# Scores of a head pair issued together in two row halves, with four bias strips, in a four-layer transformer kernel

## The reference, cut to what matters

```python
# the same pattern in moba, diff, dil (causal) and na (all 512 keys), per head h
s = einsum('bhqd,bhkd->bhqk', q, k) * 64 ** -0.5 + bias      # 64-wide contraction
s = where(mask, s, NEG)
p = softmax(s, axis=-1)
o = einsum('bhqk,bhkd->bhqd', p, v)
```

## Time and profile before

| | us |
|---|---|
| median of 3 runs | 3389.32 (3382.71 to 3393.28) |
| the profiled execution | 3389.83 |
| its span, first to last instruction | 3388.0 |
| PE busy | 3214.5 (95%) |
| POOL, DVE, ACT busy | 1659.5, 1544.9, 781.1 |

### The profile page before, as it was taken

How to read it: one execution, slowest core, us unless ns; L and a number is a source line. 1 busy time by engine, 2 the same in 40 slices (tenths; PEclk the granted TensorE clock), 3 DMA queues, 4 the chain that set the end, 5 groups by cost and what they waited for, 6 DMA issues and landing times.

```text
span 3388.0 us, 44988 instructions
## 1 busy us (share of the span) xinstructions
PE 3214.5 (95%) x14378; PEld 2530.7 (75%) x14378; DVE 1544.9 (46%) x2780; ACT 781.1 (23%) x1419; POOL 1659.5 (49%) x1254
## 2 busy tenths in 40 slices
PE   7998999999899998899999979998899999989996
PEld 5776888877688887667778858887667778868885
DVE  3335444333454434533334476633633334476634
ACT  2323221013322212142321122201142311122201
POOL 4233666662166665313246646674313256636673
PEclk9999999999999998789999989998789999979998
DMA  5225233321023232112222212232102213212232
GB/s 131 72 72 151 93 99 102 108 88 56 26 87 99 93 112 87 38 31 54 78 66 93 90 56 99 93 114 72 38 31 54 78 66 102 87 56 96 96 109 71
DMA packets 99596, 274.78 MB, mean 81 GB/s; under 512 B 38126, under 2 KB 38894, under 8 KB 99490
## 3 DMA queue, kind: packets, MB, share of 16 engines
q1 hardware_dynamic: 96176, 268.41, 24.8%
q10 hardware_dynamic: 3314, 5.02, 0.7%
HBM read 269.66 MB, written 11.54 MB: 83 GB/s over the span
## 4 chain that ended last, share of the span: by engine, by line
PE 70%; DVE 4%; ACT 1%; issue 1%; DVEq 0%; ACTq 0%
PE PA L453 10%; PE PA L455 10%; PE PA L454 10%; PE PB L453 8%; PE PB L455 8%; PE PB L454 8%; PE O L576 4%; PE S L632 3%; PE T L570 2%; PE S L539 2%; DVE acc L1194 1%; PE O L491 1%; DVE strip L1566 0%; DVE tmp L1223 0%; PE O L483 0%
## 5 line engine op out<-in xcount | busy, mean ns | idle before, releaser
L435 POOL TENSOR_TENSOR wl<-raw,wh 128x1024 fp32r<-128x1024 f32 (+2 forms) x416 | 1125.1, 2705 | 33.4
L432 POOL TENSOR_TENSOR zero<-zero 128x1 f32<-128x1 f32 x416 | 82.3, 198 | 1653.6 <-PE PA L455 799.4
L453 PE MATMUL PA<-hh,wh 128*128 128x512 f32 x1392 | 568.8, 409 | 33.9 <-DVE hl L1188 16.8
L455 PE MATMUL PA<-hh,wl 128*128 128x512 f32 x1392 | 552.6, 397 | 0.0
L454 PE MATMUL PA<-hl,wh 128*128 128x512 f32 x1392 | 552.5, 397 | 0.0
L433 POOL CAST wh<-raw 128x1024 fp32r<-128x1024 f32 (+2 forms) x416 | 478.3, 1150 | 0.0
L453 PEld LDWEIGHTS PA<-hh,wh 128*128 128x128 f32 x1392 | 266.9, 192 | 158.0 <-issue 79.0
L453 PE MATMUL PB<-hh,wh 128*128 128x512 f32 x896 | 365.0, 407 | 0.0
L454 PE MATMUL PB<-hl,wh 128*128 128x512 f32 x896 | 354.8, 396 | 0.0
L455 PE MATMUL PB<-hh,wl 128*128 128x512 f32 x896 | 354.6, 396 | 0.0
L455 PEld LDWEIGHTS PA<-hh,wl 128*128 128x128 f32 x1392 | 267.6, 192 | 58.1
(11 more groups left out here) (262 smaller groups left out, 5135.6 us busy)
## 6 DMA issues: line engine op xcount, KB each, us to landing
raw<-in_w_up SPq DMA_DIRECT2D x176, 512.0 KB, 3.4
raw<-in_w_down SPq DMA_DIRECT2D x64, 768.0 KB, 4.2
raw<-in_w_merge SPq DMA_DIRECT2D x48, 768.0 KB, 4.2
raw<-in_w_out SPq DMA_DIRECT2D x32, 512.0 KB, 3.5
strips_na<-in_rpb SPq DMA_DIRECT2D x1, 7620.0 KB, 32.0
strip<-strips_na SPq DMA_DIRECT2D x32, 224.0 KB, 4.0
strip<-strips_rel SPq DMA_DIRECT2D x96, 64.0 KB, 1.9
raw<-in_w_pool SPq DMA_DIRECT2D x12, 512.0 KB, 3.4
```

What stands on the lines that cost most here:

```text
L435: nc.gpsimd.tensor_tensor(wl[s][:, 0:width], raw[s][:, 0:width], wh[s][:, 0:width].bitcast(F), ALU.subtract).then_inc(w_split, 1)
L453: mm(dst, h_, rh, start=first, stop=False)
L455: return mm(dst, l_, rh, start=False, stop=last)
```

## The change

Within a group, unit `t` is now head `t % 2`, query tile `t // 2 % 4`. PE issues the scores of units `t` and `t+1` together at even `t`, for the same query tile of both heads, head 0 always into S0 and head 1 always into S1. The order of transposes, fill and products is otherwise that of before, by unit number. In a causal stage the units of a group now have 1, 1, 2, 2, 3, 3, 4, 4 blocks of keys.

Both strips of a group are needed from its first unit on, so a second pair of strips is made of `tmp[0]` to `tmp[3]`: even groups use `strip`, odd ones the new pair, each with its own semaphore. Their loads wait for 0, 1, 8 and 16 units taken. In `na` DVE masks the strips of the next group at `t % 8 == 4` and 5, and two of them ahead of the loop. `y_squares` writes `tmp[1]` in place of `tmp[0]`.

```diff
-        tmp = [sb(f"tmp{i}", [P, S]) for i in range(5)]
+        tmps = sb("tmps", [P, 5, S])
+        tmp = [tmps[:, i, :] for i in range(5)]
...
+        strips_at = strip, [tmps[:, 2 * i:2 * i + 2, :].rearrange("p a n -> p (a n)") for i in range(2)]
...
-                sp.wait_ge(s_taken, b["u"] + 2 if i == 0 else b["u"] + 8 * i + 4 * s - 2)
+                sp.wait_ge(s_taken, b["u"] + 2 + (0, 1, 8, 16)[i])
+                at = strips_at[i % 2][s]
...
                 def span(t):
-                    return S if full else (t % 4 + 1) * P
+                    return S if full else (t // 2 % 4 + 1) * P
+
+                def score(t):
+                    g, head, qt = t // 8, t % 2, t // 2 % 4
...
+                    if t < 2:
+                        pe.wait_ge(v_copied, 4 * b["v"] - 3 + t)
+                    pe.wait_ge(s_taken, u + t + 1)
+                    r = slice(64 * head, 64 * head + 64)
+                    mm(SB[head][:, 0:span(t)], queries[g % 2][r, qt * P:qt * P + P], keys[g % 2][r, 0:span(t)],
+                       start=True, stop=True).then_inc(s_ready, 1)
 
                 for t in range(end + 1):
-                    if t < 32:
...
-                        mm(SB[t % 2][:, 0:span(t)], queries[g % 2][r, qt * P:qt * P + P], keys[g % 2][r, 0:span(t)],
-                           start=True, stop=True).then_inc(s_ready, 1)
+                    if t < 32 and t % 2 == 0:
+                        score(t); score(t + 1)
                     if t in turns:
                         y_turn(b, turns.index(t), kind)
...
                 if full:
-                    mask_strip(0, arrived(0))
+                    mask_strip(0, 0, arrived(0)); mask_strip(0, 1, arrived(0))
                 for t in range(turns[3] + 3):
-                    g, head, qt = t // 8, t // 4 % 2, t % 4
-                    if full and t < 32 and t % 8 == 2:
-                        mask_strip(1, arrived(g))
-                    if full and t < 24 and t % 8 == 6:
-                        mask_strip(0, arrived(g + 1))
+                    g, head, qt = t // 8, t % 2, t // 2 % 4
+                    if full and t < 24 and t % 8 in (4, 5):
+                        mask_strip(g + 1, head, arrived(g + 1))
```

More of the change, by code:

```diff
@@ L70, in counts @@
     elif kind in ("causal", "na", "diff"):
-        c.update(a=3, b=3, u=32, g=4, st=4 * STRIP_PARTS[kind], d=4 * UNIT_LINKS[kind], df=4 if kind == "diff" else 0)
+        c.update(a=3, b=3, u=32, g=4, st=2 * STRIP_PARTS[kind], d=4 * UNIT_LINKS[kind], df=4 if kind == "diff" else 0)
     elif kind == "axial":
@@ L292, in build @@
         yt_ready, y_hi, y_split = sem("yt_ready"), sem("y_hi"), sem("y_split")
-        strip_in = [sem("strip_in0"), sem("strip_in1")]
+        strip_in = [[sem(f"strip_in{i}{s}") for s in range(2)] for i in range(2)]
         v_ready, v_copied = sem("v_ready"), sem("v_copied")
@@ L616, in span @@
                 def span(t):
-                    return S if full else (t % 4 + 1) * P
-                for t in range(end + 1):
-                    if t < 32:
-                        g, head, qt = t // 8, t // 4 % 2, t % 4
[L622 to L631, removed]
-                        mm(SB[t % 2][:, 0:span(t)], queries[g % 2][r, qt * P:qt * P + P], keys[g % 2][r, 0:span(t)],
-                           start=True, stop=True).then_inc(s_ready, 1)
+                    return S if full else (t // 2 % 4 + 1) * P
+                def score(t):
+                    g, head, qt = t // 8, t % 2, t // 2 % 4
+                    if t == 0:
+                        pe.wait_ge(pa_taken, b0["a"] + 2)
+                        pe.wait_ge(pb_taken, b0["b"] + 2)
+                    elif t % 8 == 0:
+                        pe.wait_ge(pa_taken, b["a"] + g + 1)
+                        pe.wait_ge(pb_taken, b["b"] + g + 1)
+                    if t < 2:
[4 more added lines that the diff above has]
+                       start=True, stop=True).then_inc(s_ready, 1)
+                for t in range(end + 1):
+                    if t < 32 and t % 2 == 0:
+                        score(t); score(t + 1)
                     if t in turns:
@@ L1303, in y_scale @@
             def y_scale(b, t, kind):
-                u, g, qt, c = b["u"], t // 8, t % 4, t % 8
-                if kind == "diff" and c >= 4:
+                u, g, qt, c, head = b["u"], t // 8, t // 2 % 4, t % 8, t % 2
+                if kind == "diff" and head:
                     link(TT(lrd[:, c:c + 1], rden[:, c:c + 1], neglam, ALU.mult))
@@ L1310, in y_scale @@
                 if kind != "diff":
-                    at = 64 * (c // 4)
+                    at = 64 * head
                     TS(y[:, at:at + 64], OB[t % 2][:, 0:64], rden[:, c:c + 1], None, ALU.mult).then_inc(o_taken, 1)
-                elif c < 4:
+                elif not head:
                     TS(y, OB[t % 2][:, 0:P], rden[:, c:c + 1], None, ALU.mult).then_inc(o_taken, 1)
@@ L1335, in y_norm, with mask_strip @@
                         ins.then_inc(y_normed, 1)
-            def mask_strip(head, at):
-                dve.wait_ge(strip_in[head], at)
-                st = strip[head][:, :].rearrange("p (j k) -> p j k", j=14)
+            def mask_strip(g, head, at):
+                dve.wait_ge(strip_in[g % 2][head], at)
+                st = strips_at[g % 2][head][:, 0:STRIP].rearrange("p (j k) -> p j k", j=14)
                 link(STT(out=st, in0=st, scalar=-1.0,
@@ L1363, in attention @@
                 if full:
[L1364 removed]
+                    mask_strip(0, 0, arrived(0)); mask_strip(0, 1, arrived(0))
                 for t in range(turns[3] + 3):
[L1366 to L1370 removed]
+                    g, head, qt = t // 8, t % 2, t // 2 % 4
+                    if full and t < 24 and t % 8 in (4, 5):
+                        mask_strip(g + 1, head, arrived(g + 1))
                     if t < 32:
                         if not full and qt == 0:
[L1373 removed]
+                            dve.wait_ge(strip_in[g % 2][head], arrived(g))
                         L = S if full else (qt + 1) * P
                         at = (6 - 2 * qt) * 64 if full else (3 - qt) * P
[L1376 removed]
+                        score(u, t, kind, L, strips_at[g % 2][head][:, at:at + L])
                     if 0 <= t - 2 < 32:
```

18 lines of the change are left out of this document (9 added, 9 removed).

## The result

| | before | after |
|---|---|---|
| median on the same chip | 3391.30 (4 runs, 3382.71 to 3393.53) | 3331.89 (4 runs, 3330.12 to 3332.65) |
| the profiled execution | 3389.83 | 3332.25 |
| its span | 3388.0 | 3330.4 |

The ratio is 0.9829, 95% interval 0.981 to 0.9847: faster by 59 us, 57.6 between the two profiled executions. The direction and two scores running at once were forecast; how much of them runs at once was not, and 3331.9 lies under the low end, 3337.

What follows compares the result with a forecast made beforehand. PE was taken to bound the kernel, busy 95% of the span. From 3389.83 us, 49.5 saved (22.9 visits, 26.6 overlap) and 7.6 of stalls added gave 3347.9, stated as 3348; range 3337 to 3379.

Steps and rivals of the forecast that it cites:

- The serial rival: Paired score passes on PE don't overlap, so the row halves do nothing: 3374.5 to 3382.5 us; chance 0.18.
- The clock's rival: Idle spells in odd steps without fill lower the granted clock, 34 us lost, 3416 with serial passes; chance 0.05.
- Part 1: In five attention stages 80 odd steps lose their separate score visit on PE: 22.9 us saved.
- behind: PE's extra time after a score, before fill matmuls run at their usual spacing: 0.11 us per visit.
- Part 2: Passes of a pair's two scores run at once in different row halves of PE: 26.6 us saved.
- A high, A low, B high, B low: PE's assumed pass order in a pair of two-pass scores A and B; only A low and B high overlap.
- from below: Bound on a pair's time on PE: one whole pass hidden per pair, no open load, 26.6 us together.
- keeps: Half of the 0.19 us inside a score, put on the second pass's weight load: 0.10 us not saved per visit.
- Part 3: New PE stalls in odd steps without fill, where a product waits for ACT's copy: 7.6 us lost.
- Steps 15 and 23: In causal stages `y_turn`'s four transposes fill 0.43 us, leaving a 0.29 us stall each; in `na` covered.
- The second mask of `na`: A 1.1 us mask on DVE before the first unit, hidden by six parts of fill (4.2 us): no cost.
- The ends of `moba`, `diff` and `dil`: Stalls in the last odd steps: `moba` 0.85, `diff` 0.15 and 0.72, `dil` 1.2 us.

Runs made afterwards that it cites:

- experiment 2: The kernel before, own unit order, with scores of units t and t+1 issued together at even t, both in the same 64 rows: 3372.78 us.
- experiment 1: The changed kernel (new numbering, strips and masks) with each score issued alone in its own step again: 3384.67 us.
- experiment 3: The changed kernel with the squares, root and norm of `diff` one step earlier: 3320.44 us.
- experiment 9: The changed kernel with both first masks of `na` ahead of the value copy on DVE: 3324.67 us.
- experiment 6: The changed kernel with the earlier norm in `diff`, ACT's copy ahead of its exponential in even steps, and `y_turn` last in its step: 3308.81 us.
- experiments 4: The changed kernel with ACT's copy of unit t-2 ahead of the exponential of unit t in even attention steps: 3332.01 us.
- 5: The changed kernel with `y_turn` last in its step, behind fill, transposes and product: 3332.12 us.
- 10: The changed kernel with the edits of experiment 6, scores paired in `axial` too, and the mask move of experiment 9: 3301.18 us.

## Where the prediction held, and why it was short by 16 us

**The mechanism held.** PE bounds the five stages, the row halves run side by side (experiment 2 against the change: 41 us), halving the visits helps on its own (16 us), and nothing else in the change matters (experiment 1). What failed is the size of the overlap and of what it gives back. The serial rival had 3374.5 to 3382.5; experiment 2 has that case, pairs whose passes don't overlap, and took 3372.8. The clock's rival had its mechanism in `diff` alone, two falls that cost about 1.4 us each where about ten were needed.

**Part 1** stands but for 4.7 of its 22.9 us. The way in and out of a pair are those of a single score, and experiment 2, net of its stalls, gained 16. But in an odd step with fill the first fill matmul now follows products instead of a score, and its neighbour starts 0.31 behind it instead of 0.23. Timeline of PE in `dil`:

```profile
797.97 1.00 PE L579 MATMUL O<-V,probsT 128*128 128x64 f32 x8
798.79 0.48 PE L456 MATMUL PB<-hh,wh 128*128 128x512 f32 x1
799.10 0.40 PE L457 MATMUL PB<-hl,wh 128*128 128x512 f32 x1
```

So of the 0.11 "behind" only 0.03 went: 59 x 0.08 = 4.7.

**Part 2 is the step that failed.** "In a pair the order is A high, A low, B high, B low", and so "one whole pass is hidden per pair". The order is not that: both heads start within 7 ns and both of B's passes are hidden, with both of its loads. A score is one matmul of the program; its two passes follow each other within its own row half and hold up nothing in the other. The bound "from below" was none: 26.6 was taken as the most that could be hidden. It is 26.6 twice, and the 0.10 that a visit "keeps" for its load was not kept for B, 80 x 0.10 = 8.0. With the 4.7 of Part 1 taken off, the gross gain worked out is 49.5 + 26.6 + 8.0 - 4.7 = 79.4.

The Trainium skill (TensorE: Matmul & The Clock Gate, The cost: per-tile semaphore tail) has increments serialize at about 26 ns each, which would have made it 2 us worse. The trace has such a tail, but PE doesn't pay it: the second increment of a pair comes 42 or 43 ns behind the first, where the passes end 7 ns apart, while a pair with two increments takes PE 1.06 and a score with one 1.05.

**Part 3 was three times too small**: 79.4 - 57.6 = 21.8 us given back, idle or at the lower clock, against 7.6. What the runs show of it:

- The wait for ACT's copy in step 7 was there: 0.8 in each causal stage (worked out: 0.72) and 0.2 in `na` (0.34), 2.8 in all.
- Steps 15 and 23 were priced at 0.29. They cost 1.0 in `moba`, `dil` and `diff`, 0.4 in `na`, because of K. This is the sentence "K is taken at DVE's step 6, and PE waits for it at step 8": step 8 was checked, but `y_turn`, which stands one step ahead of it and needs the same bank, was not. Together some 7.6 us where 1.7 was in the sum.
- In `diff` the same wait is 2.8 us, since `y_norm` on DVE, which no part of the forecast names, stands ahead of `take_k` and takes 3.8 us beside POOL's split instead of 1.3, and the clock falls behind it: 6.3 us more (experiment 3).
- The second mask of `na`, at nothing because "six parts of fill (4.2 us) lie between": two masks took 4.69 us instead of 2.2, since POOL's split runs beside them. 1.5 us in each `na`, 3.0 (experiment 9). The other masks (steps 4 and 5) collide in the same way and cost nothing, since DVE has time there.

That is 2.8 + 7.6 + 6.3 + 3.0 = 19.7 of the 21.8. The ends of `moba`, `diff` and `dil`, 2.9 in the forecast, are the rest: by PE's waits there before and after they cost 1.6, about nothing and 0.4.

A second balance agrees: 17.4 us more of idle time in the five stages, and an estimate of 4 us from the mean granted clock of the two profiled executions, 0.956 and 0.954 (0.046 of 3330.4 us less 0.044 of 3388.0). From 79.4 that leaves 58.0, against 57.6 measured.

Experiments 6 and 9 together took 19.3 + 3.0 us out of the stages by four small moves, so nearly all of it was a matter of order, not of work.

The two errors went in opposite directions: 34.6 - 4.7 = 29.9 too little gross, 14.2 too little given back. The rest, 15.7, is the miss between the sum (3347.9) and the profiled execution. That the number came so near is in part luck: each of the two errors alone would have put it 14 or 30 us off. The range's low end allowed for stalls of nothing and one hidden pass, and for no size of the gross gain above it.

## What to carry to other kernels

Fp32 matmuls that contract over 64 rows should be issued in twos, one for each half of the rows, where PE sets the pace: here the second cost nothing, passes and loads included. Where other engines are close behind, as in `axial`, less than half of PE's saving arrives (6.5 of 16.9 us). When a stage is shortened by some microseconds in steps that carry little else, follow each bank that PE writes back to the instruction that frees it, in every step, and look for what else stands ahead of that instruction, and at which of DVE's instructions will now run beside POOL's. And two mends that each show nothing in the time (experiments 4 and 5) may be worth over 10 us together, so they should be tried together before they are given up: experiment 6 less experiment 3 is 11.6 us in the medians and 13.9 in the stages, where the stages of 4 and 5 alone gave 7.4. The pair by itself was not run.

## What the runs showed of the hardware that was not expected

**DVE stopped by POOL.** The mask by line, before and after (ns, least/median/most):

```profile
L1341 DVE SCALAR_TENSOR_TENSOR strip<-strip,namask x16: 1081/1082/1490, 1594.4 to 2700.0; 128x896 f32<-128x896 f32 x16
```

```profile
L1347 DVE SCALAR_TENSOR_TENSOR strip<-strip,namask x8: 1081/1984/3168, 1568.2 to 2605.9; 128x896 f32<-128x896 f32 x8
L1347 DVE SCALAR_TENSOR_TENSOR tmps<-tmps,namask x8: 1081/1300/3980, 1580.1 to 2634.7; 128x896 f32<-128x896 f32 x8
```

The same operation on the same shape takes 1081 to 3980 ns. Before, 14 of 16 masks missed POOL's splits; after, 10 of 16 hit them. Of the masks after, each that overlaps a split (POOL's `TENSOR_TENSOR`, L438), but for the first of each `na`, takes 0.95 us plus the time that the two overlap: 0.57 of overlap makes 1.52, 2.22 makes 3.17, 3.03 makes 3.98. Such a mask does next to nothing until POOL is done. For the first, which began before the split, it is otherwise: the mask took 1.49 and POOL's split 3.12 in place of 2.40 (at 1568.16 and 1568.78).

It is not the mask alone. In this trace the scaling of one tensor (L1337) takes 2.40 in place of 0.29 with 2.31 of overlap, and `hl` (L1194), for which PE waits 17.8 us in all, up to 3.87 in place of 0.74. The instructions of DVE that read a PSUM bank keep their length: L1268 takes 0.69 on 512 columns beside a split as without. So two inputs are not needed. What is shown is where it happens and for how long; no run changed the operands to find the cause.

**The mean clock of a run decides several microseconds.** Between runs of one kernel the mean granted clock differs by a few thousandths, and the time goes with it: the kernel before took 3395.06 at 0.954 and, on another chip, 3380.52 at 0.958, about 3.6 us for 0.001; experiment 9 took 3329.59 at 0.954 and 3320.15 at 0.958. Windows of the first axial stretch, which experiment 9 doesn't touch, after and in experiment 9:

```profile
1404.90:1541.60 136.70, 130.66 (x615) 88.72 (x614) 52.42 (x160) 63.99 (x129) 19.58 (x25) 0.89 0.08 23
```

```profile
1402.30:1534.90 132.60, 125.88 (x616) 85.47 (x615) 52.43 (x160) 63.98 (x129) 19.65 (x25) 0.92 0.07 24
```

The same work, 0.89 and 0.92, 4.1 us. By that rate it would account for experiments 4 (0.953 in all four runs) and 10 (0.953 and 0.954) showing nothing in the median of what their stages gained, and for 3 (0.956 and 0.957) and 9 showing more. What sets it is open; stage lengths at a clock of 1.00 tell more of a small edit than the time does.
